# The opening of a decoder layer on one core: waits per token tile, work spread over two engines, loads from a second queue, four bank pairs

## The reference

```
h  = rms_norm(x, g_mix_pre)                 # x * rsqrt(mean(x^2) + 1e-6) * g
q, k, v, u = split(h @ w_in)                # 1024 x 2048
y1 = S5 state space over u, gelu, glu, rms_norm
y2 = differential attention over q, k, v (4 heads, ALiBi), rms_norm per head
x  = x + rms_norm(concat(y2, y1) @ w_out, g_mix_post)
x  = x + rms_norm(memory attention(rms_norm(x, g_mem_pre)), g_mem_post)
x  = x + rms_norm(swiglu(rms_norm(x, g_ffn_pre)), g_ffn_post)
```

## Time and profile before

| what | value |
| --- | --- |
| median of 3 runs | 1030.5 us (1030.44 to 1030.97) |
| profiled execution, its own time | 1034.07 us |
| its span, first to last instruction | 1032.2 us |
| PE busy | 938.9 us, 91% |
| DVE busy | 444.8 us, 43% |
| ACT busy | 362.8 us, 35% |
| POOL busy | 179.4 us, 17% |
| mean granted clock of PE | 0.959 |
| first product of `main 0` starts | 34.78 us |
| `mats_b 0` starts | 63.12 us |

### The profile page before, as it was taken

How to read it: one execution, slowest core, us unless ns; L and a number is a source line. 1 busy time by engine, 2 the same in 40 slices (tenths; PEclk the granted TensorE clock), 3 DMA queues, 4 the chain that set the end, 5 groups by cost and what they waited for, 6 DMA issues and landing times.

```text
span 1032.2 us, 17627 instructions
## 1 busy us (share of the span) xinstructions
PE 938.9 (91%) x7480; PEld 858.2 (83%) x7480; DVE 444.8 (43%) x895; ACT 362.8 (35%) x570; POOL 179.4 (17%) x45
## 2 busy tenths in 40 slices
PE   1999989787789999999869989999999999999997
PEld 1899987663369998985427979999999999999997
DVE  2699984664634488111432556322222222101013
ACT  5423223664345365135322454322222322122121
POOL 3000000000000001310001300344433334333330
PEclk9999999878789999999988989999999999999999
DMA  7214105422142156745161201222223222222212
GB/s 208 90 42 123 60 25 190 160 75 90 41 168 81 57 176 219 286 156 211 42 203 42 82 2 42 82 81 81 81 86 107 91 81 81 91 94 72 83 31 87
DMA packets 85341, 105.82 MB, mean 103 GB/s; under 512 B 9473, under 2 KB 72834, under 8 KB 85154
## 3 DMA queue, kind: packets, MB, share of 16 engines
q1 hardware_dynamic: 85282, 104.97, 30.8%
HBM read 98.26 MB, written 6.70 MB: 102 GB/s over the span
## 4 chain that ended last, share of the span: by engine, by line
PE 81%; DVE 9%; ACT 5%; issue 3%; DMA 1%; POOL 1%; SPq 0%; DVEq 0%; ACTq 0%
PE pall L1765 55%; PE pall L1777 6%; PE pall L1797 4%; PE pall L2073 2%; PE pall L2113 2%; ACT w_hi L663 1%; PE pall L2159 1%; DVE w_lo L1088 1%; PE pall L1847 1%; PE pall L2125 1%; PE pall L1950 1%; PE pall L1941 1%; PE pall L1830 1%; PE pall L1851 1%; DVE a_s L1406 1%
## 5 line engine op out<-in xcount | busy, mean ns | idle before, releaser
L626 POOL TENSOR_TENSOR w_lo<-w_raw,w_hi 128x2048 fp32r<-128x2048 f32 (+1 forms) x38 | 171.3, 4508 | 807.2 <-ACT w_hi L663 423.2
L1765 PE MATMUL pall<-x_hi,w_hi 128*128 128x272 f32 x1024 | 214.2, 291 | 2.9 <-DVE x_lo L1148 1.6
L1765 PE MATMUL pall<-x_lo,w_hi 128*128 128x272 f32 x1024 | 212.6, 289 | 0.0
L1765 PE MATMUL pall<-x_hi,w_lo 128*128 128x272 f32 x1024 | 211.4, 288 | 0.0
L1765 PEld LDWEIGHTS pall<-x_hi,w_hi 128*128 128x128 f32 x1024 | 160.9, 189 | 4.4 <-issue 1.9
L1765 PEld LDWEIGHTS pall<-x_lo,w_hi 128*128 128x128 f32 x1024 | 162.1, 190 | 0.0
L1765 PEld LDWEIGHTS pall<-x_hi,w_lo 128*128 128x128 f32 x1024 | 161.4, 189 | 0.0
L663 ACT ACTIVATE w_hi<-w_raw 128x2048 fp32r<-128x2048 f32 (+1 forms) x61 | 114.7, 1880 | 101.4 <-PE pall L1765 101.3
L1765 PE MATMUL pall<-g_hi,w_hi 128*128 128x272 f32 x352 | 73.1, 289 | 0.0
L1765 PE MATMUL pall<-g_lo,w_hi 128*128 128x272 f32 x352 | 72.6, 288 | 0.0
L1765 PE MATMUL pall<-g_hi,w_lo 128*128 128x272 f32 x352 | 72.6, 287 | 0.0
(11 more groups left out here) (373 smaller groups left out, 1609.8 us busy)
## 6 DMA issues: line engine op xcount, KB each, us to landing
w_raw<-in_w_gate SPq DMA_DIRECT2D x10, 1024.0 KB, 5.3
w_raw<-in_w_up SPq DMA_DIRECT2D x10, 1024.0 KB, 5.3
w_raw<-in_w_in SPq DMA_DIRECT2D x8, 1024.0 KB, 5.9
dm_kv<-in_cache_mem_v SPq DMA_DIRECT2D x8, 1024.0 KB, 7.2
w_raw<-in_w_down SPq DMA_DIRECT2D x8, 1024.0 KB, 5.0
w_raw<-in_w_out SPq DMA_DIRECT2D x4, 1024.0 KB, 8.6
d_k<-in_cache_k SPq DMA_DIRECT2D x16, 256.0 KB, 3.3
d_v<-in_cache_v SPq DMA_DIRECT2D x16, 256.0 KB, 3.9
```

What stands on the lines that cost most here:

```text
L626: e.tensor_tensor(w_lo[:, n % 2, 0:w], w_raw[:, n % 2, 0:w], w_hi[:, n % 2, 0:w].bitcast(F32), ALU.subtract)\
L1765: ins = mm(acc(j)[:, a, :], w, x[:, k_x + k, a * HALF:(a + 1) * HALF], start=first and k == 0 and s_, stop=last and k == kts - 1 and t_)
```

## The change

- Each of the four token tiles has a semaphore of its own, `x_in0` to `x_in3`; `x_in` keeps the sample tile (and the second load of the tokens, whose wait becomes 16 x 6).
- The 13 loads of parameter rows are issued by ACT at the start of its program, and no longer by SP.
- ACT takes a root of one number before its squares.
- ACT squares tiles 0, 1 and 4; DVE squares and sums tiles 2 and 3 with a `tensor_tensor_reduce`. ACT scales tiles 0 and 4, DVE tiles 1, 2 and 3.
- DVE writes `dt_rows` ahead of the means, after a wait for the row loads, and no longer after `par`.
- The transposes of xs use bank pairs 4, 6, 2, 0, 4, 6, 4, 6 for k = 0 to 7, with waits to match: k=2 for `dtT_ready`, k=3 for `par_ready`, k = 4 to 7 for low part 1, 2, 5 and 6.
- `main 0` no longer waits for all low parts; within its first product it waits per k for low part max(4, k + 1).
- The four semaphores of `d_v` become one, `dv_in`.

```diff
-    XS_ACT, XS_DVE = (0, 1, 4), (2, 3)
+    SQ_ACT, SQ_DVE = (0, 1, 4), (2, 3)
+    XS_ACT, XS_DVE = (0, 4), (1, 2, 3)
+    X_BANKS = (4, 6, 2, 0, 4, 6, 4, 6)
...
         for t in range(4):
-            e.dma_start(x_nat[:, t, :], x_view[:, t, :]).then_inc(x_in, 16)
+            e.dma_start(x_nat[:, t, :], x_view[:, t, :]).then_inc(S(f"x_in{t}"), 16)
...
-        (SP: the 13 loads of rows, semaphore rows_in)
...
-                    page_load(d_v, b, cv, b, [(S("s5_y"), SF)], S(f"dv_in{b}"))
+                    page_load(d_v, b, cv, b, [(S("s5_y"), SF)], S("dv_in"))
...
-        for t in range(5):
+        (ACT: the 13 loads of rows, semaphore rows_in)
+        e.wait_ge(S("eps_ready"), 1)
+        e.activation(small[:, 60:61], small[:, EPS_COL:EPS_COL + 1], ACT.Sqrt)
+        for t in SQ_ACT:
             rows = P if t < 4 else NS_TOK
-            e.wait_ge(x_in, 16 * 5)
+            e.wait_ge(*((S(f"x_in{t}"), 16) if t < 4 else (x_in, 16)))
             e.activation(xs[0:rows, t, :], x_nat[0:rows, t, :], ACT.Square, accum_out=small[0:rows, t:t + 1]).then_inc(S("x_ss"), 1)
         e.wait_ge(S("x_ms"), 2)
-        e.wait_ge(S("eps_ready"), 1)
...
-            e.activation(x_hi[:, k, :], banks(4 + 2 * (k % 2)), ACT.Copy, scale=par[:, G_MIX_PRE + k:G_MIX_PRE + k + 1])\
+            e.activation(x_hi[:, k, :], banks(X_BANKS[k]), ACT.Copy, scale=par[:, G_MIX_PRE + k:G_MIX_PRE + k + 1])\
...
         e.memset(small[:, EPS_COL:EPS_COL + 1], EPS).then_inc(S("eps_ready"), 1)
+        for t in SQ_DVE:
+            e.wait_ge(S(f"x_in{t}"), 16)
+            e.tensor_tensor_reduce(out=xs[:, t, :], in0=x_nat[:, t, :], in1=x_nat[:, t, :], scale=1.0, scalar=0.0, op0=ALU.mult, op1=ALU.add,
+                                   accum_out=small[:, t:t + 1]).then_inc(S("x_ss"), 1)
+        e.wait_ge(rows_in, 16 * N_ROW_LOADS)
+        e.tensor_copy(dt_rows[:], dt2[:].unsqueeze(2).broadcast_to([CT_N, 2, SP_])).then_inc(S("dt_rows"), 1)
         e.wait_ge(S("x_ss"), 5)
...
-            if k >= 2:
-                e.wait_ge(S("xs_lo"), k - 1)
+            if k in (2, 3):
+                e.wait_ge(*((S("par_ready"), 1) if k == 3 else (S("dtT_ready"), 1)))
+            if k >= 4:
+                e.wait_ge(S("xs_lo"), (1, 2, 5, 6)[k - 4])
...
-                if n == 0:
-                    e.wait_ge(S("xs_lo"), KT)
-                unit(n, J_W_IN + 2 * n, KT, 256, x_hi, x_lo)
+                unit(n, J_W_IN + 2 * n, KT, 256, x_hi, x_lo, ready=(lambda k: (S("xs_lo"), max(4, k + 1))) if n == 0 else None)
...
-                for b in range(4):
-                    e.wait_ge(S(f"dv_in{b}"), 32 * (n + 1))
+                e.wait_ge(S("dv_in"), 16 * PAGES * DV_N * (n + 1))
```

More of the change, by code:

```diff
@@ L452, in _ @@
         e.dma_start(ones[:], A["t_ones"]).then_inc(consts_in, 16)
[L453 to L461, removed]
         load_unit(0)
@@ L544, in _ @@
                     for b in range(DV_N):
-                        page_load(d_v, b, cv, b + DV_N, [(S("dv_done"), 1)], S(f"dv_in{b}"))
+                        page_load(d_v, b, cv, b + DV_N, [(S("dv_done"), 1)], S("dv_in"))
             elif kind == "ssm_root":
@@ L730, in ma_tail @@
                 .then_inc(S("ma_pTo"), 1)
-        for t in range(5):
+        for name, row, n in (("g_mix_pre", G_MIX_PRE, 8), ("g_mix_post", G_MIX_POST, 8), ("g_mem_pre", G_MEM_PRE, 8),
+                             ("g_mem_post", G_MEM_POST, 8), ("g_mem_kv", G_MEM_KV, 8), ("g_ffn_pre", G_FFN_PRE, 8),
+                             ("g_ffn_post", G_FFN_POST, 8), ("g_ssm_out", G_SSM, 4)):
+            e.dma_start(p_rows[row:row + n, :], A[name][0].rearrange("(k p) -> k p", p=P)).then_inc(rows_in, 16)
+        e.dma_start(p_rows[SSM_D:SSM_D + 4, :], A["ssm_d"][0].rearrange("(k g) h -> k (g h)", k=4)).then_inc(rows_in, 16)
+        e.dma_start(p_rows[G_SUB:G_SUB + 1, :], A["g_subln"]).then_inc(rows_in, 16)
+        e.dma_start(p_rows[LAM_RE:LAM_RE + 16, :], A["ssm_lam_re"][0].rearrange("(c g) s -> c (g s)", g=2)).then_inc(rows_in, 16)
+        e.dma_start(p_rows[LAM_IM:LAM_IM + 16, :], A["ssm_lam_im"][0].rearrange("(c g) s -> c (g s)", g=2)).then_inc(rows_in, 16)
+        e.dma_start(dt2[:], A["ssm_log_dt"][0].rearrange("(c g) -> c g", g=2)).then_inc(rows_in, 16)
+        e.wait_ge(S("eps_ready"), 1)
+        e.activation(small[:, 60:61], small[:, EPS_COL:EPS_COL + 1], ACT.Sqrt)
+        for t in SQ_ACT:
             rows = P if t < 4 else NS_TOK
-            e.wait_ge(x_in, 16 * 5)
+            e.wait_ge(*((S(f"x_in{t}"), 16) if t < 4 else (x_in, 16)))
             e.activation(xs[0:rows, t, :], x_nat[0:rows, t, :], ACT.Square, accum_out=small[0:rows, t:t + 1]).then_inc(S("x_ss"), 1)
         e.wait_ge(S("x_ms"), 2)
-        e.wait_ge(S("eps_ready"), 1)
         e.activation(small[:, 8:12], small[:, 8:12], ACT.Sqrt)
@@ L1140, in _ @@
         e.tensor_scalar(par[:, G_SSM:G_SSM + SF], par[:, G_SSM:G_SSM + SF], 0.5, None, ALU.mult).then_inc(S("par_ready"), 1)
-        e.tensor_copy(dt_rows[:], dt2[:].unsqueeze(2).broadcast_to([CT_N, 2, SP_])).then_inc(S("dt_rows"), 1)
         e.wait_ge(S("dtT"), 1)
@@ L1147, in _ @@
             e.wait_ge(S("xs_hi"), k + 1)
-            e.scalar_tensor_tensor(out=x_lo[:, k, :], in0=banks(4 + 2 * (k % 2)), scalar=par[:, G_MIX_PRE + k:G_MIX_PRE + k + 1],
+            e.scalar_tensor_tensor(out=x_lo[:, k, :], in0=banks(X_BANKS[k]), scalar=par[:, G_MIX_PRE + k:G_MIX_PRE + k + 1],
                                    in1=x_hi[:, k, :].bitcast(F32), op0=ALU.mult, op1=ALU.subtract).then_inc(S("xs_lo"), 1)
@@ L1809, in _ @@
                 e.wait_ge(S("xs_ready"), 5)
-            if k >= 2:
-                e.wait_ge(S("xs_lo"), k - 1)
+            if k in (2, 3):
+                e.wait_ge(*((S("par_ready"), 1) if k == 3 else (S("dtT_ready"), 1)))
+            if k >= 4:
+                e.wait_ge(S("xs_lo"), (1, 2, 5, 6)[k - 4])
             for t in range(5):
                 rows = P if t < 4 else NS_TOK
-                ins = e.transpose(banks(4 + 2 * (k % 2))[:, t * P:t * P + rows], xs[0:rows, t, k * P:(k + 1) * P], ident[0:rows, 0:rows])
+                ins = e.transpose(banks(X_BANKS[k])[:, t * P:t * P + rows], xs[0:rows, t, k * P:(k + 1) * P], ident[0:rows, 0:rows])
             ins.then_inc(S("xsT_full"), 1)
@@ L1908, in _ @@
                 if k == 0:
-                    e.wait_ge(x_in, 16 * 10)
+                    e.wait_ge(x_in, 16 * 6)
                     e.wait_ge(S("subln_t"), NH)
```

## The result

| | before | after |
|---|---|---|
| median of the runs, us | 1030.84 (1030.44 to 1030.97, 5 runs) | 1024.7 (1024.4 to 1025.63, 5 runs) |
| ratio of the times | | 0.9942 [0.9928, 0.9957] |
| profiled execution, us | 1034.07 | 1024.40 |
| its span, us; mean granted clock | 1032.2; 0.959 | 1022.6; 0.964 |
| `xs` ready, us | 19.68 | 14.35 |

The change gains 6.1 us, where 9.8 were forecast; 1024.7 lies in the range. The page's shares are those of before: what the change saved is a hole in TensorE's work, not work.

The account below looks back on a forecast made before the run. TensorE bounds the kernel, and an earlier start counts only if DVE's chain moves too. Terms: xs start 6.2, transpose pipeline 2.5, pause 1.05, sum 9.8; 1030.5 - 9.8 = 1020.7 us, range 1016.5 to 1026.5.

Parts of the forecast that it names:

- A: Opening: ACT's row-load issues become the bound, stalled beside SP's b loads; gain 3.2 us (1027.3) or 6.5 (1024); chance 0.19.
- C: Opening: a full queue blocks ACT's 13 issues repeatedly, three stalls of 4.20 us; slower by 1.5, 1032; chance 0.04.
- The pause for `w_hi 2`: DVE's chain before mats_b: its 1.05 us wait for ACT's high part of unit 2 goes, by 0.6.
- rival B's first half: Dense transposes raise TensorE's clock before product 0, which takes 12.2 us, not 14.75; gain 11.5 if it holds; rival's chance 0.15.
- The second half of B: TensorE then idles near 3.7 us before mats_b and half pace afterwards costs 2.3; gain 9.2, 1021.3; rival's chance 0.15.
- the start of `xs`: Opening: scaled tokens ready at 13.45 us instead of 19.68, worth 6.2 of the 9.8.
- dt_rows at 10.0, under ACT's 10.4: Opening, DVE: the copy of the parameter rows is done at 10.0 us, before ACT's squares end at 10.4.
- DVE has copied `par` by 14.0: Opening, DVE: the copy of par is finished by 14.0 us, before ACT's first high part ends at 15.35.
- k=3 at 18.8, none waiting: Transposes of xs: TensorE runs k=0 to 3 without waits, k=0 ending 14.84 us and k=3 18.8.
- from there on TensorE is the chain: After mats_b, starting 9.8 us earlier, TensorE bounds; DVE, ACT and loads keep their distance or are ahead.
- D: Later stretches: shifting events by 10 us can move where TensorE's clock falls; plus or minus 2 us of width, no term.
- the milder half of A: ACT's row-load issues cost 0.58 us each instead of 0.36: loss 3.3, gain 6.5, 1024.

Follow-up runs that it names:

- dt behind: The changed kernel, but DVE waits for the row loads and writes dt_rows after the reciprocals, not ahead of the means: 1027.38 us, ratio 0.9952 to the kernel before.
- both: The changed kernel with the b_pad memset also waiting for dtT_ready and dt_rows written after the reciprocals: 1024.96 us, ratio 0.9921 to the kernel before.
- two pairs: The changed kernel with two bank pairs for the transposes of xs instead of four: 1027.25 us, ratio 0.9948 to the kernel before.
- memset late: The changed kernel, but GpSimd's memset of b_pad also waits for dtT_ready: 1026.04 us, ratio 0.9937 to the kernel before.
- before again: The kernel before, unchanged, run and profiled a second time: 1033.19 us, ratio 1.0007.
- after again: The changed kernel, unchanged, run once more on another chip: 1027.0 us, ratio 0.9944 to the kernel before.
- both, again: The kernel of "both" run once more, unchanged: 1022.84 us, ratio 0.991 to the kernel before.
- low part behind b_pad: The kernel of "both", but DVE writes the low part of unit 2 behind the first b_pad: 1028.78 us, ratio 0.9958 to the kernel before.
- page reads later: The kernel of "low part behind b_pad", but SP reads the page table after unit 7's load, not unit 4's: 1022.72 us, ratio 0.9895 to the kernel before.

## Why the prediction was right or wrong

**Right:** what bounds the kernel and that only DVE's chain and TensorE's together carry an earlier start to the end. By its steps:
- ACT's 13 issues: 5.2 us from 0.74 to 5.92, forecast 4.7; none over 0.59. Root at 7.25, forecast done at 7.0. Square needed no table. DVE's square 1.22 and 1.23, forecast 1.23 from the slope of the earlier trace rows.
- Rivals A and C fell. The second b load did stall SP, for 6.42, but it was issued at 6.04, when ACT's issues were over. ACT issuing while SP is stalled did not arise and stays untested. That the stall is a full queue, as the prediction has it, no row shows; the rows show an issue of 4.20 and of 6.42 us.
- Squares to scale: 10.65 to 11.52 in "dt behind", where `dt` is out of the way (0.87, forecast 0.85).
- The pause for `w_hi 2` went: the low part of unit 2 follows at 44.49 without idle time. Last low part to the end of `b_pad` 27.32, forecast 27.28.
- Product 0 began at half pace, so rival B's first half fell. The Trainium skill, "TensorE: Matmul & The Clock Gate", section "What's actually happening", has activity of TensorE release the throttled clock; the transposes of this opening did not do it, not even in "both", where they filled 10.36 of the 10.70 us ahead of product 0.
- The second half of B, a loss of clock in front of `mats_b`, was seen once, at 2.55 idle, and not at 1.57, 1.59, 1.93 or the 2.16 of "two pairs". Its price of 2.3 was misread: in before the granted clock was at 0.50 from 184 to 188 us already, ahead of the matmul at 188.96. The one case here cost 1.6.

**Wrong, a term mis-sized: the start of `xs`, 6.2 in the sum.** It came 0.85 less. 0.2 is the squares' end (10.60 for 10.4); 0.6 is the step "dt_rows at 10.0, under ACT's 10.4". I costed the row loads by their issue and took their landing for granted; `dt` landed 5.64 after its issue, while tokens and weights kept the DMA engines busy (busy share 1.07 from 4.00 to 11.20 us), and DVE's means stood behind it. Which of these transfers held it no run isolates. "dt behind" shows this part: 0.60 at the means, 0.6 at `mats_b`.

**Wrong, a step left out: "DVE has copied `par` by 14.0", "k=3 at 18.8, none waiting".** The copy was in time; the scaling behind it wasn't, because the memset of `b_pad` started in the same moment. In before the memset also began when `xs` was ready, and the scaling had been over 1.5 us earlier. The change moved `xs` forward past it. It cost about 1.0 at product 0 and at `mats_b`; "memset late" and "both" show it. The Trainium skill, "SBUF — State Buffer", section "Who interferes with whom", says that a DVE scaling or copy in its two-port mode and a GpSimd instruction exclude each other for the whole of the one that has the ports. I had not weighed that rule. The trace agrees for the scaling, 3.50 beside 3.52; that it was in that mode, no row shows. The copy reads PSUM and stands behind the scaling in DVE's order, so whether the memset or the scaling held it stays open.

So 9.8 - 0.85 - 1.0 = 7.95 at `mats_b`, and 8.0 was measured against the profiled execution of before (7.0 against the one of before again).

**Wrong, the way from `mats_b 0` to the end: from 8.0 to 6.1.** The prediction said it would take a difference between openings and subtract it from the median, since "from there on TensorE is the chain" and all else keeps its distance. The traces compare the same matmuls in each kernel (start, us):

| | before | before again | after | after again | dt behind | both, again |
|---|---|---|---|---|---|---|
| product 0 | 34.78 | 34.51 | 26.09 | 26.07 | 25.50 | 24.51 |
| `mats_b 0` | 63.12 | 62.10 | 55.11 | 55.07 | 54.52 | 53.49 |
| seventh matmul of `main 4` | 94.38 | 94.13 | 86.68 | 86.63 | 86.78 | 85.21 |
| 16 small matmuls (L2035, later L2042 or L2043) | 208.21 | 207.11 | 199.55 | 199.96 | 200.93 | 198.01 |
| span | 1032.2 | 1030.3 | 1022.6 | 1023.0 | 1025.5 | 1021.0 |
| mean granted clock | 0.959 | 0.964 | 0.964 | 0.961 | 0.959 | 0.964 |

First, the gap in front of `main 4`'s seventh matmul evens out what the openings differ by. In before the opening varies by 1.0 at `mats_b 0`, since there the pace of `main 0` reaches DVE's chain through `w_hi` 2, and by 0.25 behind the gap. The change is worth 7.0 or 8.0 at `mats_b 0`, depending on the execution of before, and 7.45 to 7.75 behind the gap.

Second, the whole span follows the clock, and two executions of one kernel part between 189 and 212 us. At clocks 0.959 and 0.964 the medians of the spans differ by 7.25 and 7.05, while the medians over all executions differ by 6.1, and by 5.8 where both were run again. Before has 9 executions of 43 at 0.966 and after has none of 11: that is where I put the difference, and no run isolates it. It fits that the five executions of before behind the 6.1 took 1030.44 to 1030.97, where those at 0.966 took 1029.70 to 1030.88 and those at 0.964 took 1030.70 to 1032.68; their own clocks are not on record. The prediction gave this (D) a width and no sign. What sets the clock's level of an execution I could not find. "Dt behind" sat at 0.959 six times out of six, and before, beside it on the same chip, twice out of 17, so chance alone is a poor account of it; that none of 11 of after reached 0.966 could be chance.

**The range held partly by luck.** 1024.7 lies 4.0 above the forecast time, in the part of the range that was there for the milder half of A. A did not happen. What filled its place, the hold on `par`, the landing of `dt` and the clock, was not in the sum.

What each part is worth at `mats_b 0`, by taking it alone away: bank pairs 1.9, the split of squares and scalings 1.5, rows 0.5, the wait for each k 0.0. The early root, the waits for each tile, the order of `par` and `dt` and the merged `dv_in` were not undone singly; with the pause of 1.05 they hold the remaining 4.1 of the 8.0, if the parts add, which the split and the hold show they don't quite.

## What to carry to other kernels

A step that is moved forward meets whatever was timed by the same event: list what else its semaphore releases, and on which engines, before counting the gain. Cost a small load by its landing and by what stands in order behind its wait, not by its issue. When the profile is of one execution, ask first how far its opening, and its clock, stand from the others'. And follow a gain past its first landmark: the 0.6 of "dt behind" was there at `mats_b 0` and gone 32 us later.

## What the runs showed of the hardware

- A 128x4 scaling on DVE and a 128x16 copy out of PSUM took 3.50 and 3.43 us beside a 3.52 us memset on GpSimd, and 0.17 where it began after them. But DVE's next instruction in order, the low part of unit 0, ran its usual 2.29 from 16.12, beginning inside that time. The record of both held instructions ends with the memset; DVE was not shut for it.
- 16 reads of the page table on SP take 30 us, 1.85 each ("low part behind b_pad", 54.31 to 83.86); whatever stands behind them in the queue is that late.
- 10.33 us of transposes between 14.35 and 26.00 did not bring product 0 to the full pace: it began with 24 starts in 5 us. The windows print a granted clock of 1.00 for both. The trace's record of the clock begins only at 30.63 in after and 40.26 in before, within 0.1 us of where the half pace ends, so ahead of it the count of starts has to be read, not the clock.
- The 13 row loads cost 0.28 to 0.59 us each to issue on ACT's queue, and 0.25 to 0.42 on SP's.
- The seventh matmul of `main 4` is preceded by a gap put down to "issue": 0.30 in before, 1.08 in before again, 0.62 in after, 1.34 in "dt behind" and none in "page reads later". It follows a 16 KB packet of the DMA queue that the profile calls "instruction": the packet ends at 93.11, 92.75, 85.16 and 85.33 in the first four, and the matmul starts 1.27, 1.38, 1.52 and 1.46 later. In all 11 traces with this gap the distance is 1.27 to 1.52, while the gap itself is 0.30 to 1.34; in "page reads later" the packet was there 1.97 before the matmul. So TensorE most likely waits for its own instructions here. No run moved that packet by itself.
